# Out-projection of the second half of the tokens turned to tokens on partitions, in column blocks

## The reference

```
h    = RMSNorm(x) * norm_gain
proj = h @ w_in            # RWKV-7 group and sliding-window attention group
mix  = concat(y_rwkv, y_attn)         # (1024, 2048)
x    = x + mix @ w_out                # w_out is 2048 x 2048
out  = x * rsqrt(mean(x*x over the 2048 channels) + 1e-5) * final_gain
```

## Time and profile before

| what | value |
|---|---|
| median of 3 executions | 1868.52 us (1866.35 to 1871.46) |
| the profiled execution: span from first to last instruction | 1866.2 us |
| the profiled execution's own time | none is listed apart from its span; the fastest timed execution is 1866.35 |
| TensorE busy | 1836.8 us, 98% |
| VectorE, ScalarE, POOL busy | 67%, 42%, 25% |
| DMA | 207.69 MB, mean 111 GB/s |

### The profile page before, as it was taken

How to read it: one execution, slowest core, us unless ns; L and a number is a source line. 1 busy time by engine, 2 the same in 40 slices (tenths; PEclk the granted TensorE clock), 3 DMA queues, 4 the chain that set the end, 5 groups by cost and what they waited for, 6 DMA issues and landing times.

```text
span 1866.2 us, 38160 instructions
## 1 busy us (share of the span) xinstructions
PE 1836.8 (98%) x15008; PEld 1496.9 (80%) x15008; DVE 1245.1 (67%) x2255; ACT 788.6 (42%) x1578; POOL 467.9 (25%) x1096
## 2 busy tenths in 40 slices
PE   8999999999999999999999999999999999999996
PEld 5878888888888887888888888888888788878885
DVE  4676777777777678667777777677777754355333
ACT  6444444343534355444343534353534543242221
POOL 0005051423324150041423324150505060111110
PEclk9999999999999999999999999999999999999998
DMA  5533232333233325332333333333333543465443
GB/s 182 167 109 101 90 94 84 97 93 89 91 93 96 89 91 177 106 89 85 97 92 89 91 92 96 89 92 90 96 89 98 174 127 108 124 206 172 156 126 124
DMA packets 194963, 207.69 MB, mean 111 GB/s; under 512 B 98272, under 2 KB 101472, under 8 KB 194784
## 3 DMA queue, kind: packets, MB, share of 16 engines
q1 hardware_dynamic: 194784, 205.26, 36.8%
HBM read 183.18 MB, written 22.02 MB: 110 GB/s over the span
## 4 chain that ended last, share of the span: by engine, by line
PE 93%; DVE 4%; ACT 1%; DMA 1%; issue 1%; SPq 0%; DVEq 0%; ACTq 0%
PE psum L1184 76%; PE psum L1169 3%; PE psum L1313 2%; PE psum L1248 2%; PE psum L1286 1%; PE psum L1466 1%; PE psum L1347 1%; PE psum L1430 1%; PE psum L1273 1%; PE psum L1437 1%; PE psum L1210 1%; PE psum L1193 1%; DVE w_lo L754 1%; PE psum L1419 1%; DVE work L873 1%
## 5 line engine op out<-in xcount | busy, mean ns | idle before, releaser
L1184 PE MATMUL psum<-x_hi,w_hi 128*128 128x512 f32 x2144 | 871.7, 407 | 11.3 <-DVE x_lo L763 6.7
L1184 PE MATMUL psum<-x_hi,w_lo 128*128 128x512 f32 x2144 | 837.8, 391 | 0.0
L1184 PE MATMUL psum<-x_lo,w_hi 128*128 128x512 f32 x2144 | 837.1, 390 | 0.0
L754 DVE TENSOR_TENSOR w_lo<-w_raw,w_hi 128x512 fp32r<-128x512 f32 x536 | 371.6, 694 | 498.5 <-ACT w_hi L549 470.7
L549 ACT ACTIVATE w_hi<-w_raw 128x512 fp32r<-128x512 f32 x536 | 335.3, 629 | 774.9 <-PE psum L1184 692.3
L1184 PEld LDWEIGHTS psum<-x_hi,w_hi 128*128 128x128 f32 x2144 | 403.1, 188 | 111.3 <-issue 14.4
L1184 PEld LDWEIGHTS psum<-x_hi,w_lo 128*128 128x128 f32 x2144 | 402.6, 188 | 87.7
L1184 PEld LDWEIGHTS psum<-x_lo,w_hi 128*128 128x128 f32 x2144 | 403.6, 188 | 79.0 <-issue 4.1
L504 POOL TENSOR_TENSOR sub_t<-sub_l,sub_io 128x60 f32<-128x60 f32 (+24 forms) x496 | 187.4, 378 | 876.8 <-DMA sub_l<-scratch_L 839.2
L506 POOL TENSOR_TENSOR sub_io<-sub_io,sub_t 128x60 f32<-128x60 f32 (+24 forms) x496 | 201.6, 406 | 38.8
L526 POOL TENSOR_TENSOR v<-v,kb 128x512 f32<-128x512 f32 x29 | 38.3, 1321 | 266.4 <-ACT kb L698 266.1
(11 more groups left out here) (241 smaller groups left out, 1816.7 us busy)
## 6 DMA issues: line engine op xcount, KB each, us to landing
w_raw<-in_w_in SPq DMA_DIRECT2D x408, 256.0 KB, 2.6
w_raw<-in_w_out SPq DMA_DIRECT2D x128, 256.0 KB, 2.6
sub_l<-scratch_L SPq DMA_DIRECT2D x16, 512.0 KB, 4.4
stage<-in_x_t SPq DMA_DIRECT2D x20, 256.0 KB, 3.3
stage<-scratch_MIX SPq DMA_DIRECT2D x19, 256.0 KB, 3.5
late<-in_x_t SPq DMA_DIRECT2D x16, 256.0 KB, 3.1
scratch_MIX<-sa SPq DMA_DIRECT2D x16, 256.0 KB, 4.0
scratch_MIX<-ym SPq DMA_DIRECT2D x16, 256.0 KB, 3.2
```

Of the source, the lines that this page charges most:

```text
L754: nc.vector.tensor_tensor(w_lo[gq % SPLIT][:], w_raw[gq % RAW][:], w_hi[gq % SPLIT][:].bitcast(F32), ALU.subtract).then_inc(w_ready, 1)
L1184: mm = nc.tensor.matmul(psum[:, s % 2], wt[gq % SPLIT][:, cols], xx[:, c], start=(c == 0 and wt is w_hi and xx is x_hi), stop=(c == KC - 1 ...
```

## The change

The second half of the out-projection is computed with tokens on partitions. The stationary operand is a 128-token piece of `x_hi` or `x_lo`, the moving one a weight unit, which now is 128 input channels by 512 output channels (`w_rows`). The output is cut into column blocks `cb` of 512 channels and token blocks `tb` of 128 tokens: 16 pieces, one PSUM bank each. There are five passes over the 16 units of a column block: three of them do all four token blocks (12 matmuls a unit), and the last column block is done in two passes, with token blocks 0, 1 and then 2, 3 (6 matmuls a unit). So 80 units are loaded and split where there were 64. The number of matmuls stays 768.

At the end of a pass VectorE adds the residual to each piece (`add_rows`), ScalarE squares it with a running sum along the row (`accum_out`), POOL multiplies the pieces of the first three column blocks by the gain. After the last column block of a token block: sum of four numbers per row, root, reciprocal, and the scaling by one number per row, two pieces on ScalarE and two on VectorE. The last four units of the last pass are held back (`last_rows`): TensorE waits for all of them, then finishes token block 2, then 3.

```diff
+CBS = D // HALF
+TBS = HALF // P
+PASSES = [(cb, range(TBS)) for cb in range(CBS - 1)] + [(CBS - 1, (0, 1)), (CBS - 1, (2, 3))]
+LAST_UNITS = 4
+QUARTERS = ROWS + KC * len(PASSES)
+PIECES = [(cb, tb) for cb, tbs in PASSES for tb in tbs]
...
+def row_bank(cb, tb):
+    return (0 if cb % 2 else 4) + tb
... SP
+                def residual_rows(n):
+                    cb, tb = PIECES[n]
+                    if n < 2:
+                        sp.wait_ge(tile_read, OUT0 + KC)
+                    else:
+                        sp.wait_ge(row_read, n - 1)
+                    sp.dma_start(x_in[n % 2], io["x_rows"][...]).then_inc(row_in_landed[n % 2], 16)
+                def residual_rows_at(gq):
+                    for n in range(len(PIECES)):
+                        end = 0
+                        for at, (cb, tbs) in enumerate(PASSES):
+                            begin, end = end, end + len(tbs)
+                            if begin <= n < end:
+                                early = n - begin < 2
+                                if gq - ROWS == KC * at + (10 + n - begin if early else KC):
+                                    residual_rows(n)
...
+                    if gq == ROWS + 4:
+                        sp.wait_ge(x_ready, 4 * KC)
+                        sp.dma_start(gain_row, io["gain_row"]).then_inc(row_gain_landed, 16)
+                    if gq >= ROWS:
+                        residual_rows_at(gq)
+                    if gq >= ROWS + 9 and gq - ROWS - 9 < KC:
+                        store(gq - ROWS - 9)
+                    if gq == ROWS + 4 * KC + 6:
+                        store_rows(0)
+                        store_rows(1)
+                store_rows(2)
+                store_rows(3)
... POOL
+                def gain_rows(cb):
+                    pool.wait_ge(row_gain_landed, 16)
+                    for tb in range(TBS):
+                        pool.wait_ge(row_squared, TBS * cb + tb + 1)
+                        nc.gpsimd.tensor_tensor(piece, piece, gain_row[...], ALU.mult).then_inc(row_gained, 1)
... ACT, in loop gq, after high(gq + 4)
+                    if gq >= ROWS + KC and (gq - ROWS) % KC == 0:
+                        cb, tbs = PASSES[(gq - ROWS) // KC - 1]
+                        for tb in tbs:
+                            square_rows(PIECES.index((cb, tb)))
+                        if cb == CBS - 1:
+                            for tb in tbs:
+                                root_rows(tb)
+                            for tb in tbs:
+                                scale_rows(tb)
+                for tb in (2, 3):
+                    square_rows(PIECES.index((CBS - 1, tb)))
+                    root_rows(tb)
+                    scale_rows(tb)
... DVE, in loop gq, after low(gq + 4)
+                    if gq >= ROWS + KC and (gq - ROWS) % KC == 0:
+                        cb, tbs = PASSES[(gq - ROWS) // KC - 1]
+                        dve.wait_ge(w_used, gq)
+                        for tb in tbs:
+                            add_rows(PIECES.index((cb, tb)))
+                    if gq == ROWS + 4 * KC:
+                        for tb in (0, 1):
+                            sum_rows(tb)
+                        for tb in (0, 1):
+                            invert_rows(tb)
+                        for tb in (0, 1):
+                            scale_rows(tb)
+                for tb in (2, 3):
+                    dve.wait_ge(row_full, tb - 1)
+                    add_rows(...); sum_rows(tb); invert_rows(tb); scale_rows(tb)
... PE
+                def row_products(gq, tb, c, cb):
+                    nc.tensor.matmul(psum[:, bank], x_hi[:, c, tokens], hi[:], start=(c == 0), stop=False)
+                    nc.tensor.matmul(psum[:, bank], x_hi[:, c, tokens], lo[:], start=False, stop=False)
+                    return nc.tensor.matmul(psum[:, bank], x_lo[:, c, tokens], hi[:], start=False, stop=(c == KC - 1))
+                def rows(gq):
...
+                    if at == 0:
+                        pe.wait_ge(x_ready, 3 * KC + c + 1)
+                    if at == 1 and c == 0:
+                        pe.wait_ge(tile_read, OUT0 + KC)
+                        pe.wait_ge(c_rooted, 1)
+                    if at in (2, 3) and c == 0:
+                        pe.wait_ge(row_read, TBS * (at - 1))
+                    pe.wait_ge(w_ready, gq + 1)
+                def last_rows():
+                    pe.wait_ge(w_ready, QUARTERS)
+                    for tb in tbs:
+                        for n in range(LAST_UNITS, 0, -1):
+                            mm = row_products(QUARTERS - n, tb, KC - n, cb)
+                        mm.then_inc(row_full, 1)
...
-                pe.wait_ge(c_summed, 2 * KC - 1)
-                for last, squared in enumerate((c_acc[:], c_sq[(2 * KC - 1) % 2])):
...
-                pe.wait_ge(c_spread, 1)
...
-                dve.wait_ge(c_turned, 1)
-                for t in range(KC):
-                    scale(1, t)
```

More of the change, by code:

```diff
@@ L257, in program @@
                       pt[:, 0], pt[:, 1]]]
+        row_piece = [[xn[1][CBS * tb + cb] for cb in range(CBS)] for tb in range(TBS)]
+        row_inv = stat[:, 0, 0:TBS]
         psum = ctx.enter_context(nc.psum_tensor("psum", [P, 8, HALF], F32))
@@ L541, in _ @@
                                 clear(j - 1)
-                    for u in range(2 * KC - 1):
+                    for u in range(KC):
                         if gq == done(OUT0 + u) + 1:
                             accumulate(u)
+                    for at in range(CBS - 1):
+                        if gq == ROWS + KC * (at + 1):
+                            gain_rows(at)
             @block.scalar
@@ L734, in _ @@
                             channels(j, at)
-                    for u in range(2 * KC - 1):
+                    for u in range(KC):
                         if gq == done(OUT0 + u) + 1:
                             square(u)
[L738 to L741, removed]
+                    if gq == ROWS + 5:
+                        root()
+                    if gq >= ROWS + KC and (gq - ROWS) % KC == 0:
[11 more added lines that the diff above has]
+                    scale_rows(tb)
             @block.vector
@@ L1103, in scale, with invert @@
[L1103 to L1106, removed]
+                    nc.vector.tensor_tensor(xn[0][u], psum[:, (OUT0 + u) % 2], x_in[u % 2], ALU.add
+                                            ).then_inc(tile_read, 1)
+                def invert():
+                    dve.wait_ge(c_rooted, 1)
+                    then(nc.vector.reciprocal(rms[0][:], rms[0][:]))
@@ new lines, in sum_rows, with invert_rows, scale_rows @@
+                def sum_rows(tb):
+                    dve.wait_ge(row_squared, PIECES.index((CBS - 1, tb)) + 1)
+                    nc.vector.tensor_reduce(row_inv[:, tb:tb + 1], row_sums[:, tb], AX, ALU.add).then_inc(row_summed, 1)
+                def invert_rows(tb):
+                    dve.wait_ge(row_rooted, tb + 1)
+                    then(nc.vector.reciprocal(row_inv[:, tb:tb + 1], row_inv[:, tb:tb + 1]))
+                    dve.sem_inc(row_inverted, 1)
+                def scale_rows(tb):
+                    inv = row_inv[:, tb:tb + 1]
+                    dve.wait_ge(row_gained, TBS * (CBS - 1))
+                    nc.vector.tensor_scalar(row_piece[tb][2], row_piece[tb][2], inv, None, ALU.mult
+                                            ).then_inc(scaled_by_dve, 1)
+                    nc.vector.scalar_tensor_tensor(row_piece[tb][3], row_piece[tb][3], inv,
+                                                   gain_row[:, 3 * HALF:], ALU.mult, ALU.mult
+                                                   ).then_inc(scaled_by_dve, 1)
@@ L1486, in between @@
                                 chain(j - 1, 2 * (at - 20))
-                    quarter(gq, between)
-                pe.wait_ge(c_summed, 2 * KC - 1)
-                for last, squared in enumerate((c_acc[:], c_sq[(2 * KC - 1) % 2])):
[L1491 to L1496, removed]
-                pe.wait_ge(c_spread, 1)
-                for b in range(NB):
-                    mm = turn(psum[:, 3, b * P:(b + 1) * P], rms[0][:, b * P:(b + 1) * P])
-                mm.then_inc(c_turned, 1)
+                    if gq < ROWS:
+                        quarter(gq, between)
+                    else:
+                        rows(gq)
+                last_rows()
 SCRATCH = {
```

148 lines of the change are left out of this document (98 added, 50 removed).

## The result

| | before | changed |
|---|---|---|
| median of 5 executions | 1867.37 us | 1874.80 us |
| range | 1866.35 to 1871.46 | 1874.37 to 1876.24 |
| ratio, 95% interval | | 1.0040 [1.0027, 1.0052] |
| span of the profiled execution | 1866.2 | 1872.6 |

The change makes the kernel 0.4% slower, 7.4 us by the medians. The forecast was 1870.0, its range 1860.5 to 1876.5. Its mechanisms are there, one by one; in the second half their sizes together were some 7 us too small, and a part ahead of it, which the change does not touch, happened to be 2.2 us shorter. The time of an execution is some 2 us longer than its span (1874.6 and 1872.6 us for the profiled one).

The account below looks back on a forecast made before the run. TensorE, 98% busy, plus a 17.7 us tail were taken as the bound. Span 1854.1 with the shorter tail, plus 1.8 + 4.65 + 5.5 + 1.6, gave 1867.7; with 2.3 for timed runs, 1870.0 us, range 1860.5 to 1876.5.

Parts of the forecast that it names:

- The start and the matmuls: Start of the second half: the 1.7 us stall goes; the 768 matmuls keep their rate, 0.2267 us each.
- The tail: Behind the last matmul: chain 3.6, block 3 late 0.9, last scaling to end 2.8; 7.3 us against 17.7.
- End of pass 2: Residuals, adds and squares delay the next split; TensorE stalls 1.8 us, then units arrive just in time.
- Cover gone about 0.3 us: End of pass 2: a VectorE scaling slowed beside POOL's product takes about 0.3 us of cover.
- The clock behind it: After the first long stall: half clock not added, as TensorE waits for weights again anyway.
- the wait at the end of pass 3: Adds, squares, roots and scalings of two token blocks stand before unit 69's split; TensorE stalls 4.65 us.
- End of pass 4: Before the last held-back matmuls: eight stores in SP's queue delay loads 77 to 79; stall taken as 5.5 us.
- The ring-order rule: End of pass 4: DMA engines consume descriptors in ring order; by that alone the stall is 6.1 us.
- The last wait's clock: Behind the last wait: the 24 held-back matmuls lose 1.6 us to half clock, the middle of nothing and 3.3.
- rival 1: Lead survives, tail's gain kept: 1861 to 1863 us, with no stall at all 1856.4; chance 0.22, faster.
- Rival 2: Thin passes: loads land late, over the 2.66 us break-even; from 3.15 us time exceeds 1874.1; chance 0.18, slower.
- Rival 3: Tail as long as before, block 3 waiting for its residual or the last stores; 1873 us; chance 0.05.

Follow-up runs that it names:

- one-pass form: Against the changed kernel: last column block in one pass of 12 matmuls a unit, 64 units instead of 80, stores behind the last weight load; 1857.86 us.
- e5_warm: Changed kernel with 30 matmuls into an unused PSUM bank, never read, placed before TensorE's last wait for weights; 1873.93 us.
- e4_raw4: Changed kernel with a fourth raw buffer from the last unit of pass 2 on; 1870.91 us.
- e6_raw4_stores_last: Changed kernel with both a fourth raw buffer and the eight stores of token blocks 0 and 1 behind the last weight load; 1863.97 us.
- e1_stores_last: Changed kernel with the eight stores of token blocks 0 and 1 issued behind the last weight load, not behind unit 76's; 1869.99 us.
- e3_spread_adds: Changed kernel with the four adds and squares ending passes 0 to 2, and the later two residual loads, spread over four loops; 1875.62 us.
- e7_one_pass_five: Last column block in one pass, with five units held back instead of four and the first token block waiting for each unit; 1855.81 us.

## Why the prediction came out as it did

**The number.** 1874.8 lies inside the range and 4.8 us above the forecast. By the mark that the prediction set itself, 5.6 us, the kernel is slower (7.4 us by the medians), and to that it had given 0.25, against 0.53 for no change. It named the three places where TensorE would wait, and what releases it there; none of the waits had the length that it gave: 3.6 us for 1.5 to 2, 2.65 for 4 to 5, 7.9 for 4 to 6.

**The start and the matmuls: right.** No wait for a bank at the start of the second half; matmuls every 0.2267 us with the operands' roles swapped (1669.32 to 1669.54 to 1669.77). In the one-pass form the matmuls take 175.0 us in all.

**The tail: right in its chain, short in its end.** The last block's chain is 3.44 us (1864.72 to 1868.16) for the 3.6 predicted, 0.84 late for 0.9. But from the last scaling to the end it takes 4.4 us, not 2.8: four stores become ready within 0.8 us (1867.51 to 1868.29) and go out one after the other.

```profile
1867.42 0.74 DVE L1218 SCALAR_TENSOR_TENSOR pt<-pt,stat,kw 128x512 f32<-128x512 f32 x1
```

```profile
1867.71 0.94 SPq L484 DMA_DIRECT2D out_rows<-score  x2
1868.70 0.96 SPq L484 DMA_DIRECT2D out_rows<-pt  x2
```

The last store goes out about 1869.2, 1 us behind the scaling; before, it followed within 0.1. The other 0.6 is the landing, 3.0 us in the median of the last two where it was 2.4. Tail 8.7 instead of 7.3. Mis-sized by 1.4.

**End of pass 2: right place, 3.6 for 1.8 us.** VectorE, the changed kernel:

```profile
1802.91 0.68 DVE L1201 TENSOR_TENSOR sub_l<-psum,decay 128x512 f32<-128x512 f32 x1
1806.54 0.69 DVE L1201 TENSOR_TENSOR gs<-psum,lora 128x512 f32<-128x512 f32 x1 [2.94 <-DMA lora<-in_x_rows]
1807.71 0.69 DVE L1201 TENSOR_TENSOR pt<-psum,decay 128x512 f32<-128x512 f32 x1 [0.49 <-DMA decay<-in_x_rows]
1809.71 2.59 DVE L852 TENSOR_TENSOR w_lo<-w_raw,w_hi 128x512 fp32r<-128x512 f32 x3 [1.31 <-ACT w_hi L619]
```

The residuals landed 3.5 and 4.1 us after their issue, where 2.9 was taken; and the first low part took 1.40 us (1809.71 to 1811.11 in the chain that ended last), POOL's product running beside it. "Cover gone about 0.3 us" was the wrong size: it was 0.7. In e5_warm, the same code up to here, the wait was 2.17 us. There the last residual landed after at most 3.5 us, not 4.1, and the low part was not held up; POOL's product beside it took 1.74 us instead of 1.27:

```profile
1807.00 0.69 DVE L1201 TENSOR_TENSOR gs<-psum,lora 128x512 f32<-128x512 f32 x1 [2.91 <-DMA lora<-in_x_rows]
1807.61 0.69 DVE L1201 TENSOR_TENSOR pt<-psum,decay 128x512 f32<-128x512 f32 x1
```

So this term differs between executions, and with it whether the clock falls: with waits of 3.5 to 3.6 us (the changed kernel, e4_raw4, e6_raw4_stores_last) it fell, with 2.3 us (e1_stores_last, e5_warm) it did not.

**The clock behind it: the step stood.** The prediction had left half clock out of the sum before the last wait, since TensorE would wait for weights again anyway. It cost 2.6 us there, the wait at the end of pass 3 was 2.65 us instead of 4.65, and the splits themselves were where they were foreseen: low 68 to low 69 took 6.3 us (1831.98 to 1838.24), 6.4 predicted. Units came every 1.39 us in pass 3 (1811.11 to 1831.98, 15 units), 1.34 predicted. e3_spread_adds shows the same from the other side. Two more executions bear it out. In e1_stores_last and e5_warm, the same code up to here, the clock stayed full behind the first wait, and yet TensorE went on with unit 69 no more than 0.3 to 0.5 us sooner: 168.6 and 168.4 us after its first matmul of the second half, where it was 169.0 in the changed kernel. They waited 4.1 and 4.0 us there, near the 4.65 of the prediction. TensorE in e5_warm:

```profile
1838.23 0.50 PE L1601 MATMUL psum<-w_hi,x_hi 128*128 128x512 f32 x1 [3.89 <-DVE w_lo L852]
```

So up to unit 69 what failed is the supply alone: low 69 ended 37.2 us after the end of pass 2, where the prediction's steps add up to 35.1. Of the 2.1 us, 1.5 are the work at the end of pass 2 (low 53 at 10.1, not 8.6) and 0.7 the slower units.

**End of pass 4: right cause, 7.9 for 5.5 us.** This is the largest error of a single term. e1_stores_last shows that the stores are the cause. The step that failed is the issue time, "0.43 us each": eight stores in a row took 0.67 each, 5.3 us, so the loads behind went out 1.9 us later than worked out and landed after 4.4 us; the issue of these three loads, 1.88 us together, adds another 0.5. In the window of 1845 to 1850 us the DMA engines were busy all the time (share 1.03, 392 GB/s); that SP had to wait for them to drain is argued from that, not shown. The ring-order rule of the Trainium skill, DMA: Bandwidth & Descriptors, section Queues, rings and completion order, gave 6.1, nearer than the value taken; it says nothing of the time that SP needs.

**The last wait's clock: 2.5 for 1.6 us.** By the profile of e5_warm it is real. The Trainium skill, TensorE: Matmul & The Clock Gate, section Why this matters for your kernels, warns of idle gaps between bursts, and the trace agrees: the granted clock is 0.50 behind the first and the last wait.

Together: last wait +2.4, the first wait +1.8 and its clock +2.6 less 2.0 at the wait behind it, clock at the end +0.9, tail +1.4: 7.1 us more than the sum, less the 2.2 us of the untouched part: 1872.6, where 1867.7 was predicted. In this list "+1.8, +2.6 less 2.0" is one error, the 2.1 us of late supply, and not three. That the untouched part took 2.2 us off is luck. The rivals: a second half without a wait, the far end of rival 1, was seen only in the one-pass form. Rival 2, late loads in the thin passes, was a small part of it: the loads landed after 2.8 us in the median, not 3.15, but over the break-even of 2.66, and that is the 0.7 us of pass 3. Rival 3 did not happen.

## What to carry to other kernels

A pass that halves the matmuls per unit of weights also halves the time in which the next unit must be loaded and split. Compare that time with the round trip of one buffer divided by their number before anything else; here 1.36 against 1.34 us predicted and 1.39 measured, and every piece of work placed ahead of a split then shows up in full. To shorten a tail, hold back the last products of a full-width pass (e7_one_pass_five), rather than run a thin pass. Where stores and loads share one queue, issue the loads that the bound engine waits for first.

## What the runs showed of the hardware that was not expected

- In the changed kernel the clock fell sooner than in the kernel before: 2.3 us (1807.58 to some 1809.88) and 2.8 us (1848.01 to some 1850.85) after the last matmul slot, against 4.5. A wait of 2.65 us (1835.64 to 1838.29) left it full. Behind both half-clock waits 12 matmuls were slow.
- The fall can come after the wait. In e5_warm TensorE went on at full clock at 1838.23, behind its wait of 4.0 us, and the granted clock fell to half only at some 1839.51 (windows as above):

```profile
1839.00:1840.00 1.00, 1.00 (x5) 0.78 (x4) 0.38 (x1) 0.00 (x0) 0.00 (x0) 0.76 0.67 199
```

- Issuing a store took SP 0.43 us at first and 0.67 on average in a row of eight.
- A 128x512 subtraction on VectorE with both inputs in SBUF took 1.40 to 1.43 us (1.78 in e4_raw4) when it started behind a POOL product that was still running, 0.69 alone.
